# Output projection of three token blocks in rounded parts, and seven expert-table remainders moved to GpSimd, in an encoder block with a PEER expert layer

## The chip, the cores and the metric

The kernel runs on one core of a Trainium2 chip. The metric is the device time of one execution in microseconds (us), taken over several runs; a profile shows one more execution, instruction by instruction. The engines are named as in the profile: PE (TensorE, matmuls), DVE (VectorE), ACT (ScalarE), POOL (GpSimd) and SP (SyncE, which only issues transfers here).

## The reference

One encoder block on 512 tokens of width 1024: a mixer (a recurrent group with 8 heads in both directions and a short gated convolution with 4 channel groups), its output projection, a layer norm, a product-key expert layer (PEER), and a second layer norm.

```python
def reference(x, ...):
    h = layer_norm(x, ln_emb_g, ln_emb_b)
    z = h @ w_in
    xr, gate, cb, cc, cx = jnp.split(z, IN_SPLITS, axis=-1)
    ...
    y_lru = gelu(gate) * lru                      # 1024 channels
    y_conv = cb * depthwise_conv(cc * cx, conv_w) # 512 channels
    mix = jnp.concatenate([rms_norm(y_lru, norm_lru_g), rms_norm(y_conv, norm_conv_g)], -1)
    h = layer_norm(ALPHA * h + mix @ w_out, ln1_g, ln1_b)
    f = peer(h, peer_wq, peer_k1, peer_k2, peer_u, peer_v)
    h = layer_norm(ALPHA * h + f, ln2_g, ln2_b)

def peer(x, w_q, k1, k2, u_tab, v_tab):
    # per token and head (8 heads): the 16 best of 128 x 128 expert pairs, softmax g
    act = gelu(einsum("cd,ced->ce", x, u_tab[idx]))
    return einsum("ce,ced->cd", g * act, v_tab[idx])
```

## The kernel before, in words

The 512 tokens are four blocks of 128 (TB = 4). Everything is float32, but most products are made in rounded parts: a tile x is split into x_hi (x copied to the rounded matmul type by ACT) and x_lo (the remainder x - x_hi, also rounded, by DVE or POOL), and a product is a_hi b_hi + a_hi b_lo + a_lo b_hi, three rounded matmuls. The output projection is the exception: there `mm` takes the whole float32 tiles.

The program is four stages, each written as one list of instructions per engine; there is no scheduler, and each engine runs its list in order and waits on semaphores.

**Mixer** (`mixer`). For each of 28 column chunks of w_in: load (SP), upper part (ACT), remainder (POOL, `w_lower`, L401), 24 matmuls (`z_chunk`, L729). The results, 12 channel chunks, stand in `y` (chunks 0 to 7 are the heads, 8 to 11 the convolution; they are finished in the order `made`, convolution first). At the end of each head DVE runs two scans (L673), then POOL's `head_output` adds them, multiplies by the gate into `y` and squares (L409, L411, L416). The output projection (L772 to L791) goes block by block: 4 convolution chunks x 2 halves of 512 columns (L776), then 8 head chunks x 2 halves (L787); each matmul has a 128x128 piece of `y` as weights and 512 columns of `wo` as moving data. In block 0 it waits for the last head, and the sums of squares (L753, into bank 2) come before its last chunk. The mean squares go to DVE (L680) and POOL (L441). Block tb + 2 uses the banks of block tb, so it waits until DVE has added block tb's banks to `h` (L692, `o_used`); after that come statistics, POOL's root (L810, L812) and `normalise` (L557).

**Queries** (`queries`). The four blocks are turned into `xhi`, `xlo`; then 16 steps of one query chunk (24 matmuls, L1294), one block of 128 rows of the table U (128 blocks in all), and scores; 3 more steps have a U block only. A U block m: load into `u_raw` (4 buffers, L842), 8 transposes into PSUM (`turn`, L868), upper part by ACT (L897), remainder, 24 matmuls with 384 moving columns (`product`, L880), gelu, store. The transposes of block m + 1 stand ahead of the products of block m, and wait for the remainders of block m (each half for its bank). In this stage the remainder is made by POOL (`lower`, L920), which cannot read PSUM, so ACT writes a second, whole copy of each half (L900). DVE picks the top 16 of each score row meanwhile. The first four U blocks and the keys are loaded as soon as the mixer's buffers are free; the vectors `ln1_g`, `ln1_b` after the last block's `o_used`.

**Gates** (`gates`). 77 steps s, U block 19 + s each. Here the remainders are made by DVE straight from PSUM (`lower_pair`, L938). DVE also does the selection for each block (steps `SELECT_AT`: the far block 3 at 0 to 2, block 2 at 3 to 6, block 0 at 7 to 10, block 1 at 30 to 33), the one-hot tiles of two blocks (19 steps from 11 and from 43), and products of gathered rows. The far block is not made through the dense tables: POOL gathers its 128 rows per token of U and later of V (`GatherPath`, L1040, ring of 4 tiles), and DVE multiplies (`use`, L1052, L1056). `EARLY_USES` says how many of these uses stand in the query stage, `U_FROM` how many are done when the gate stage ends. From step 7 (`SCATTER_AT`) POOL also scatters the gates of block 2 to memory (L231). PE needs block 0's selection at the end of step 10.

**Experts** (`experts`). 128 steps over the table V with rounded parts (L1687), 32 of them with a U block as well; two gathered rows are used a step, later one. In step `WEIGH` (the first in which 128 uses are done) the gates are multiplied by the gelus and the two sums are cleared, and the uses of V rows begin.

## Time and profile before

| what | value |
|---|---|
| time of the kernel, median of 3 runs | 1699.42 us (1698.40 to 1699.64) |
| the profiled execution's own time | 1702.07 us |
| its span, first to last instruction | 1700.3 us |
| mean granted TensorE clock | 0.991 of full speed |
| PE busy | 96% |
| DVE busy | 74% |
| POOL busy | 49% |
| ACT busy | 38% |

Spans and times are of one execution. A matmul's record is longer than the distance to the next (they are pipelined), so costs of series are read from the chain of work or from the distance between starts. A whole float32 matmul leaves two records.

### The profile page before, as it was taken

How to read it: one execution, taken by the hardware profiler on the slowest of the kernel's cores; microseconds unless marked ns; L12 is line 12 of the kernel's file. 1: busy time of each engine (PE TensorE's matmuls, PEld its weight loads, DVE VectorE, ACT ScalarE, POOL GpSimd, SP SyncE). 2: the span in 40 equal slices, each digit the busy share in tenths (PEclk: the TensorE clock that was granted, in tenths of full speed). 3: DMA queues.
4: the chain of work that ended last, by engine and by line, in shares of the span. 5: the costliest groups of instructions: out<-in, count | busy, mean ns of one | idle time of the engine just before them, and what ended most of it. 6: DMA issues, size and time to landing. Idle time of an engine off the chain costs nothing.

```text
span 1700.3 us, 23332 instructions
## 1 busy us (share of the span) xinstructions
PE 1635.7 (96%) x8522; PEld 1418.6 (83%) x8522; DVE 1257.8 (74%) x2452; ACT 647.8 (38%) x1062; POOL 828.5 (49%) x542
## 2 busy tenths in 40 slices
PE   7998999899998999999999889999999999999997
PEld 5876644499998999999999888888888888888885
DVE  6567853388998898855886357778777877888876
ACT  3558750332433433432433233333333333333332
POOL 4734421274443378877877424445555563222200
PEclk9999999999999999999999999999999999999999
DMA  8436311133335578798779989998999989999973
GB/s 273 150 97 191 109 36 54 50 118 118 97 123 179 157 212 227 225 322 240 213 221 272 351 301 330 320 325 319 320 326 322 323 297 341 357 352 358 354 254 112
DMA packets 242896, 397.15 MB, mean 234 GB/s; under 512 B 33704, under 2 KB 173408, under 8 KB 242784
## 3 DMA queue, kind: packets, MB, share of 16 engines
q1 hardware_dynamic: 182816, 259.17, 44.8%
q0 software_dynamic: 55296, 134.31, 26.0%
q10 hardware_dynamic: 4672, 2.19, 0.5%
q8 instruction: 68, 1.11, 0.3%
q14 instruction: 44, 0.36, 0.1%
HBM read 349.40 MB, written 46.20 MB: 233 GB/s over the span
## 4 chain that ended last, share of the span: by engine, by line
PE 75%; DVE 14%; ACT 5%; DMA 2%; issue 2%; ACTq 1%; POOL 0%; SPq 0%; DVEq 0%; POOLq 0%
PE bank L1687 30%; PE bank L880 24%; PE bank L868 5%; PE bank L729 5%; PE bank L787 3%; PE bank L1561 3%; PE bank L1294 2%; DMA u_raw<-in_peer_u 2%; DVE dq L669 1%; PE bank L776 1%; DVE hd L673 1%; DVE sel_late L989 1%; ACT dw L536 1%; ACT da L538 1%; DVE ut_lo L938 1%
## 5 line engine op out<-in xcount | busy, mean ns | idle before, releaser
L880 PE MATMUL bank<-xhi,ut_hi 128*128 128x384 f32 x1024 | 354.8, 346 | 0.3 <-ACT gel L906 0.3
L880 PE MATMUL bank<-xhi,ut_lo 128*128 128x384 f32 x1024 | 344.7, 337 | 0.0
L880 PE MATMUL bank<-xlo,ut_hi 128*128 128x384 f32 x1024 | 344.0, 336 | 0.0
L1040 POOL DMA_INDIRECT gathered<-in_peer_v,expert_rows x128 | 198.2, 1549 | 261.5 <-DVE gather_sum L1056 242.6
L1040 POOL DMA_INDIRECT gathered<-in_peer_u,expert_rows x128 | 171.0, 1336 | 192.5 <-DVE gather_product L1052 167.0
L938 DVE TENSOR_TENSOR ut_lo<-bank,ut_hi 128x512 fp32r<-128x512 f32 x216 | 141.5, 684 | 154.4 <-ACT ut_hi L897 127.3
L231 POOL DMA_INDIRECT gate_matrix<-gate_values,gate_cells x128 | 221.1, 1728 | 56.5 <-issue 37.2
L1687 PE MATMUL bank<-v_hi,w_hi 128*128 128x512 f32 x760 | 237.7, 394 | 1.3 <-DVE w_lo L1799 1.3
L1687 PE MATMUL bank<-v_hi,w_lo 128*128 128x512 f32 x760 | 234.9, 390 | 0.0
L1687 PE MATMUL bank<-v_lo,w_hi 128*128 128x512 f32 x760 | 234.6, 390 | 0.0
L1732 ACT ACTIVATE v_hi<-gate_rows_then_feed 128x1024 fp32r<-128x1024 f32 x128 | 135.4, 1059 | 235.2 <-PE bank L1687 235.2
L1782 DVE TENSOR_TENSOR v_lo<-gate_rows_then_feed,v_hi 128x1024 fp32r<-128x1024 f32 x128 | 156.5, 1222 | 51.6 <-ACT v_hi L1732 51.6
L880 PEld LDWEIGHTS bank<-xhi,ut_hi 128*128 128x128 f32 x1024 | 193.8, 189 | 0.5 <-issue 0.5
L880 PEld LDWEIGHTS bank<-xlo,ut_hi 128*128 128x128 f32 x1024 | 193.9, 189 | 0.0
L880 PEld LDWEIGHTS bank<-xhi,ut_lo 128*128 128x128 f32 x1024 | 193.1, 189 | 0.0
L897 ACT ACTIVATE ut_hi<-bank 128x512 fp32r<-128x512 f32 x256 | 145.3, 604 | 84.6 <-PE bank L868 82.1
L1687 PEld LDWEIGHTS bank<-v_hi,w_lo 128*128 128x128 f32 x760 | 142.9, 188 | 30.0
L1687 PEld LDWEIGHTS bank<-v_lo,w_hi 128*128 128x128 f32 x760 | 142.9, 188 | 30.0
L1052 DVE SCALAR_TENSOR_TENSOR gather_product<-gathered,h 128x1024 f32<-128x1024 f32 x128 | 156.0, 1219 | 14.1 <-DMA gathered<-in_peer_u,expert_rows 9.6
L1687 PEld LDWEIGHTS bank<-v_hi,w_hi 128*128 128x128 f32 x760 | 140.8, 189 | 29.3 <-issue 1.7
L868 PE MATMUL bank<-ident,u_raw 128*128 128x128 f32 x1024 | 140.2, 275 | 23.6 <-DVE ut_lo L938 11.2
L1056 DVE SCALAR_TENSOR_TENSOR gather_sum<-gathered,expert_gates,gather_sum 128x1024 f32<-128x1024 f32 x128 | 160.5, 1278 | 0.3 <-DMA gathered<-in_peer_v,expert_rows 0.3
(212 smaller groups left out, 2515.2 us busy)
## 6 DMA issues: line engine op xcount, KB each, us to landing
u_raw<-in_peer_u SPq DMA_DIRECT2D x128, 512.0 KB
gate_rows_then_feed<-in_peer_v SPq DMA_DIRECT2D x128, 512.0 KB
gate_rows_then_feed<-gate_matrix SPq DMA_DIRECT2D x128, 192.0 KB
activations<-gel SPq DMA_DIRECT2D x96, 192.0 KB
gate_rows_then_feed<-activations SPq DMA_DIRECT2D x96, 192.0 KB
u_raw<-in_w_in SPq DMA_DIRECT2D x28, 512.0 KB, 4.1
gate_matrix<-gate_zeros SPq DMA_DIRECT2D x8, 1024.0 KB, 6.9
wq<-in_peer_wq SPq DMA_DIRECT2D x16, 512.0 KB, 4.6
```

What stands on the lines that cost most here:

```text
L231: self.nc.gpsimd.indirect_dma_start(out=self.flat, out_offset=bass.IndirectOffsetOnAxis(ap=self.at[:, k:k + 1], axis=0), in_=self.gate[:, ...
L729: ins = mm(z_bank(n)[:, :], w[n % 2][:, k, :], x[:, k, :], start=(i == 0), stop=(i == 3 * KD - 1))
L868: ins = self.nc.tensor.transpose(self.bank[b][:, k * P:(k + 1) * P], raw[:, j * P:(j + 1) * P], self.ident[:, :])
L880: ins = self.nc.tensor.matmul(self.bank[b + (r % 2) * spare][:, 0:DTOK], u[r % 2][:, k, :], x[:, k, 0:DTOK], start=(i == 0), stop=(i == 3 ...
L897: ins = self.nc.scalar.activation(self.hi[r % 2][at], turned, ACT.Copy)
L938: self.nc.vector.tensor_tensor(out=self.lo[r % 2][at], in0=self.bank[b].rearrange("p (k e) -> p k e", k=4), in1=self.hi[r % 2][at].bitcast ...
L1040: self.nc.gpsimd.indirect_dma_start(out=self.tile[r][:, :], out_offset=None, in_=self.tables[kind], in_offset=bass.IndirectOffsetOnAxis(ap ...
L1052: ins = V.scalar_tensor_tensor(out=self.product[:, :], in0=self.tile[r][:, :], scalar=1.0, in1=self.x, op0=ALU.mult, op1=ALU.mult, accum_o ...
L1056: ins = V.scalar_tensor_tensor(out=y, in0=self.tile[r][:, :], scalar=self.gate[:, k:k + 1], in1=y, op0=ALU.mult, op1=ALU.add)
L1687: ins = mm(bank[2 + 2 * tb + half][:, :], w[r][:, tb * P:(tb + 1) * P], v[r][:, half * HALF_D:(half + 1) * HALF_D], start=begins, stop=ends)
L1732: S.activation(v_hi[r][:, :], v_raw[r][:, :], ACT.Copy).then_inc(v_hi_ready, 1)
L1782: V.tensor_tensor(out=v_lo[r][:, :], in0=v_raw[r][:, :], in1=v_hi[r][:, :].bitcast(F32), op=ALU.subtract).then_inc(v_lo_ready, 1)
```

## The change

1. **Projection.** Blocks 1 to 3 are projected in rounded parts: ACT makes `wo_hi` and `y_hi` of each chunk (1024 and 384 columns), DVE's new `wo_lower` the remainders in place of `wo` and of blocks 1 to 3 of `y`. Block 0 stays whole, and so does one half of block 1's convolution chunks (`whole(1, 1, c, 1)`), which now stands ahead of block 0's heads. The upper parts lie in `xhi`, `xlo`, `ut_hi`, `ut_lo` and `u_raw`.
2. **Loads.** Since `u_raw` is in use, the first four U loads wait for the last block's `o_used`; they stand ahead of the loads of `ln1_g` and `ln1_b`. `prow` shares the buffer of `conv_products`, and its clearing waits for the transposes of `prow`.
3. **Gathers.** The query stage uses 4 gathered rows (`EARLY_USES` 2 and 2 instead of 2 and 4), the gate stage 71 instead of 70, the expert stage one more. With `U_FROM` odd, the use of the first V row falls into the step ahead of `WEIGH`, so the clearing of the sums drops that row's product (one of 128 per token of the far block).
4. **Remainders.** In steps 0 to 6 of the gate stage POOL makes the remainders (`lower`), ACT the second copies (`upper`).

```diff
-EARLY_USES = (0,) * (QC - 1) + (2, 4)
+EARLY_USES = (0,) * (QC - 1) + (2, 2)
...
+        eng.wait_ge(pT_ready, 1)
         G.memset(prods[:, :], 0.0).then_inc(prods_zero, 1)
...
+        for i, c in enumerate(made):
+            S.activation(wo_hi[c], wo[:, c, :], ACT.Copy).then_inc(wo_hi_ready, 1)
+            eng.wait_ge(y_ready, i + 1)
+            S.activation(y_hi[c], y[:, c, P:T], ACT.Copy).then_inc(y_hi_ready, 1)
...
+        def wo_lower(i):
+
+            eng.wait_ge(wo_hi_ready, i + 1)
+            eng.wait_ge(chunk_used, i + 1)
+            c = made[i]
+            V.tensor_tensor(out=wo_lo[c], in0=wo[:, c, :], in1=wo_hi[c].bitcast(F32),
+                            op=ALU.subtract).then_inc(wo_lo_ready, 1)
+            eng.wait_ge(y_hi_ready, i + 1)
+            eng.wait_ge(sq_ready, i + 1)
+            V.tensor_tensor(out=y_lo[c], in0=y[:, c, P:T], in1=y_hi[c].bitcast(F32),
+                            op=ALU.subtract).then_inc(y_lo_ready, 1)
+
+        for i in range(MIX // 2):
+            wo_lower(i)
         eng.wait_ge(sums_done, MIX)
...
         ins.then_inc(ms_ready, 1)
+        for i in range(MIX // 2, MIX):
+            wo_lower(i)
...
+            if tb == 1:
+                at = made.index(c) + 1
+                eng.wait_ge(wo_lo_ready, at)
+                eng.wait_ge(y_lo_ready, at)
+            tok = slice((tb - 1) * P, tb * P)
+            for ya, wb, begins, ends in ((y_hi[c][:, tok], wo_hi[c], first, False),
+                                         (y_hi[c][:, tok], wo_lo[c], False, False),
+                                         (y_lo[c][:, tok], wo_hi[c], False, last)):
+                for half in halves:
+                    ins = mm(out_bank(tb, i, half)[:, :], ya, wb[:, half * HALF_D:(half + 1) * HALF_D],
+                             start=begins, stop=ends)
...
+        for c in range(HEADS, MIX):
+            whole(1, 1, c, 1, c == HEADS, c == MIX - 1).then_inc(chunk_used, 1)
+        eng.wait_ge(factors_ready, 2 * HEADS)
...
+        mixed.out_used(eng, TB - 1)
         for m in range(UB):
             acts.load(eng, m, m)
-        mixed.out_used(eng, TB - 1)
...
         def gpsimd(eng):
             for s in range(STEPS):
+                if s < BY_POOL:
+                    acts.lower(eng, BY_QUERIES + s + 1, BY_QUERIES + s + 1)
                 for q in range(started_by(s), started_by(s + 1)):
                     far.start(eng, q)
```

On DVE, between the last head's scan and the first addition to `h`, before:

```order
L669 TENSOR_TENSOR dq<-dq,th 128x512
L673 SCALAR_TENSOR_TENSOR hd<-da,dq 128x512
L680 TENSOR_SCALAR rms<-bank 128x4 x2
L692 SCALAR_TENSOR_TENSOR h<-bank,rms,h 128x512 x4
L551 BN_STATS bn<-h 128x6 x2
```

The same place after (`wo_parts` and `y_parts` are the remainders, `ut_hi`, `xhi`, `y_hi`, `u_raw_parts` the places of the upper parts):

```order
L698 SCALAR_TENSOR_TENSOR hd<-da,dq 128x512
L708 TENSOR_TENSOR wo_parts<-wo,ut_hi 128x1024
L712 TENSOR_TENSOR y_parts<-y,y_hi 128x384
...
L708 TENSOR_TENSOR wo_parts<-wo,xhi 128x1024
L712 TENSOR_TENSOR y_parts<-y,u_raw_parts 128x384
L719 TENSOR_SCALAR rms<-bank 128x4 x2
L708 TENSOR_TENSOR wo_parts<-wo,xhi 128x1024
L712 TENSOR_TENSOR y_parts<-y,u_raw_parts 128x384
...
L733 SCALAR_TENSOR_TENSOR h<-bank,rms,h 128x512 x4
```

Six pairs now stand ahead of the mean squares and six between them and the first addition to `h`.

On POOL, from the last query remainders to the first scatters, before:

```order
L1230 TENSOR_TENSOR wq_lo<-wq,wq_hi 128x1024
L920 TENSOR_TENSOR ut_lo<-gather_sum,ut_hi 128x512 x4
L1040 DMA gathered<-in_peer_u,expert_rows 128x1024 x2
L920 TENSOR_TENSOR ut_lo<-gather_sum,ut_hi 128x512 x6
L1040 DMA gathered<-in_peer_u,expert_rows 128x1024 x5
L231 DMA gate_matrix<-gate_values,gate_cells 6291456x1 x6
```

The same place after:

```order
L1296 TENSOR_TENSOR wq_lo<-wq,wq_hi 128x1024
L986 TENSOR_TENSOR ut_lo<-gather_sum,ut_hi 128x512 x12
L1106 DMA gathered<-in_peer_u,expert_rows 128x1024 x4
L986 TENSOR_TENSOR ut_lo<-gather_sum,ut_hi 128x512 x12
L1106 DMA gathered<-in_peer_u,expert_rows 128x1024
L232 DMA gate_matrix<-gate_values,gate_cells 6291456x1 x6
```

Two gathers no longer stand among the query stage's remainders; four gathers now stand between the remainders of gate steps 0 and 1, and 14 halves of remainders (steps 0 to 6) are new.

## Rows read from the trace of the kernel before

**Rows 1.** The page: busy time by engine, and the chain by engine.
```profile
PE 1635.7 (96%) x8522; PEld 1418.6 (83%) x8522; DVE 1257.8 (74%) x2452; ACT 647.8 (38%) x1062; POOL 828.5 (49%) x542
PE 75%; DVE 14%; ACT 5%; DMA 2%; issue 2%; ACTq 1%; POOL 0%; SPq 0%; DVEq 0%; POOLq 0%
```
**Rows 2.** The chain of work, from 234 us: start, length, what (times and lengths in us).
```profile
234.45 12.28 PE bank L787 x28
248.41 1.82 PE bank L787 x4
...
298.31 13.75 PE bank L787 x32
...
588.77 4.17 PE bank L880 x24
...
749.21 0.87 PE bank L868 x8
...
1022.93 8.20 PE bank L1687 x36
```
**Rows 3.** Timeline of DVE: start, length, line, count, [idle before, releaser].
```profile
118.04 0.69 DVE L669 TENSOR_TENSOR dq<-dq,th 128x512 f32<-128x512 f32 x1 [0.93 <-ACT dq L495]
...
119.91 2.78 DVE L669 TENSOR_TENSOR dq<-dq,th 128x512 f32<-128x512 f32 x1
...
239.01 1.22 DVE L673 TENSOR_TENSOR_SCAN hd<-da,dq 128x512 f32<-128x512 f32 x1
...
250.81 2.85 DVE L692 SCALAR_TENSOR_TENSOR h<-bank,rms,h 128x512 f32<-128x512 f32 x4 [2.13 <-POOL rms L441]
...
549.34 2.29 DVE L980 TENSOR_TENSOR hit_late<-placef_late,iotab_late 128x2048 bf16<-128x2048 bf16 x1
...
1209.10 1.22 DVE L1782 TENSOR_TENSOR v_lo<-gate_rows_then_feed,v_hi 128x1024 fp32r<-128x1024 f32 x1
1210.23 0.55 DVE L1799 TENSOR_TENSOR w_lo<-w,w_hi 128x384 fp32r<-128x384 f32 x1
1210.70 0.69 DVE L938 TENSOR_TENSOR ut_lo<-bank,ut_hi 128x512 fp32r<-128x512 f32 x1
```
**Rows 4.** Timeline of POOL, the same columns.
```profile
119.48 2.66 POOL L403 TENSOR_TENSOR ut_lo<-u_raw,ut_hi 128x1024 fp32r<-128x1024 f32 x1 [11.16 <-ACT ut_hi L469]
...
240.37 1.26 POOL L409 TENSOR_TENSOR hd<-hd 128x512 f32<-128x512 f32 x1 [10.51 <-DVEq L676]
...
248.76 2.01 POOL L441 TENSOR_TENSOR rms<-rms,small 128x4 f32<-128x4 f32 x2 [4.67 <-DVE rms L680]
...
331.22 2.49 POOL L920 TENSOR_TENSOR ut_lo<-gather_sum,ut_hi 128x512 fp32r<-128x512 f32 x2 [13.72 <-ACT gather_sum L900]
...
529.15 1.88 POOL L1040 DMA_INDIRECT gathered<-in_peer_u,expert_rows  x1 [2.13 <-DVE gather_product L1052]
...
534.00 0.94 POOL L1040 DMA_INDIRECT gathered<-in_peer_u,expert_rows  x1 [0.30 <-issue]
```
**Rows 5.** Timeline of ACT: its first work behind the mixer's heads.
```profile
252.76 1.06 ACT L1200 ACTIVATE wq_hi<-wq 128x1024 fp32r<-128x1024 f32 x1 [15.90 <-DMA wq<-in_peer_wq]
```
**Rows 6.** Transfers issued from 313 to 331 us: KB each, us to landing.
```profile
ln<-in_ln_b SPq DMA_DIRECT2D x1, 512.0 KB, 5.5
wq<-in_peer_wq SPq DMA_DIRECT2D x1, 512.0 KB, 6.6
```
**Rows 7.** Timeline of PE: the projection's start, and the waits where the gate stage opens.
```profile
226.64 7.03 PE L776 MATMUL bank<-wo,y 128*128 128x512 f32 x16
...
516.82 0.63 PE L868 MATMUL bank<-ident,u_raw 128*128 128x128 f32 x4 [0.79 <-POOL ut_lo L920]
...
538.11 1.94 PE L868 MATMUL bank<-ident,u_raw 128*128 128x128 f32 x8 [5.22 <-DVE ut_lo L938]
```
**Rows 8.** Busy time by stretch: PE, PEld, DVE, ACT, POOL, then granted clock, DMA share, GB/s.
```profile
538.00:541.00 3.00, 2.89 (x12) 2.92 (x13) 2.93 (x4) 1.19 (x2) 0.00 (x0) 0.50 0.84 338
...
600.00:995.00 395.00, 384.81 (x2563) 381.13 (x2563) 274.93 (x588) 138.03 (x325) 287.06 (x187) 1.00 0.89 256
```

80 lines of the change are left out of this document (52 added, 28 removed).

## The prediction

> **What bounds the kernel now.** I read the page first: PE is busy 96% of the span and holds 75% of the chain [rows 1]. So a change pays where it shortens PE's own work or takes away one of its few waits. Then I read the chain around the projection and the gate stage [rows 2], the timelines of the engines that feed PE there [rows 3, 4], and PE's waits [rows 7]. The reader should see three things. From 234.45 to 312.05 us PE does almost nothing but whole float32 matmuls, back to back [rows 2]. From 516 us, where the gate stage opens, it waits for remainders, above all 5.22 us at 538.11 [rows 7]. And the granted clock is at the lower level (0.50 of 2.4 GHz, so 1.2 GHz) right behind that wait [rows 8].
>
> All times below are in the old trace's coordinates. Where both changes act, the later one simply starts earlier by what the first one gained, since the query stage starts when the projection ends and nothing in it hangs on an absolute time.
>
> **1. The matmuls of the projection.** 32 records are 16 whole matmuls in 13.75 us, 0.859 us each [rows 2]. The same form in rounded parts (128x128 weights, 512 moving columns, two halves on one weight tile) takes 8.20 us for 36, 0.228 us each, three of them 0.683 [rows 2]. So a matmul saves 0.176 us. Changed are 24 in block 2, 24 in block 3, 20 in block 1: 68 x 0.176 = 11.9 us. The four whole matmuls that are pulled ahead of block 0's heads (3.4 us) use up PE's wait of 0.8 us for the last factors of the heads: the convolution part of block 0 ends at 226.64 + 7.03 = 233.7, the heads' part begins at 234.45 [rows 2, 7]. Ideal: 12.7 us.
>
> **2. The remainders on DVE, and who waits.** A 1024-column remainder starts 1.13 us before the next instruction, a 384-column one 0.47 us (1209.10, 1210.23, 1210.70) [rows 3]: 1.60 a pair, 12 pairs, 19.3 us. They can start when DVE's last scan ends, at 240.2. ACT is free from 236.9 (15.90 us before 252.76), and its 1024-column copy takes 1.06 us [rows 5], the 384-column one less, so ACT stays ahead. Block 0 ends at 248.41 + 1.82 [rows 2] + 3.4 - 0.8 = 252.9 us.
>
> There is a catch. A DVE instruction with two SBUF inputs that met a POOL one (start 119.48, end 122.14) took 2.78 us instead of 0.69: it was over 0.55 us after POOL's end [rows 3, 4]. The two alternate. The first six pairs meet POOL's three instructions of `head_output` from 240.37 on (1.26 us the first [rows 4], 3.6 in all), so they end at 240.2 + 9.6 + 3.6 = 253.4; with the mean squares about 253.8. PE may open block 1 (whose bank 2 holds them) 0.9 us late. The other six pairs meet POOL's roots (2.01 us [rows 4]): 253.8 + 9.6 + 2.0 = 265.4. Inside block 1 PE needs 2.7 us for the convolution halves and 1.37 us for each head chunk, DVE 1.60 to 1.9; DVE is two chunks ahead when it begins, and its last remainder (265.4) is due at 253.8 + 2.7 + 7 x 1.37 = 266.1. No stall, but no more than 0.7 us of room. Block 1 ends at 267.4. Then block 2 waits for DVE's addition of block 0, 2.85 us, which stood at 250.81 [rows 3] and now is queued behind the pairs: 265.4 + 2.9 = 268.3, so 0.9 us more. Later additions fit (a block takes 16.4 us on PE). Projection: 12.7 - 1.8 = **10.9 us** saved. Bounds: without any collision 12.7; with each DVE instruction at its full record (1.22 + 0.55 = 1.77 a pair) two more, 8.9.
>
> The Trainium skill speaks against both halves of the change here: "GPSIMD Engine Reference", Key points, says that GpSimd shares its SBUF interfaces with VectorE and contends with instructions that have two SBUF inputs. By it the new pairs contend, and the gate remainders, which DVE took from PSUM, become contending ones on POOL. The trace agrees with it for the pair at 119.48. Without the rule the projection would give its 12.7.
>
> **3. Loads.** The four U loads now wait for the last `o_used`, which comes 2.9 us after the projection's end, at 315. PE needs the first of them, and POOL the norm vectors, shortly before POOL's remainder at 331.22 [rows 4]. Two of the loads issued there, 0.5 us apart, landed 5.5 and 6.6 us after issue, 1.6 us apart [rows 6]. With four more in front the U blocks land by 325 and the vectors by 327. Cost nothing, under the projection's tail (norm, turn, first query chunk); 4 us of room. The `prow` wait and the one gathered row more in the gate and expert stages lie under other work (DVE is busy 74% [rows 1]).
>
> **4. Opening of the gate stage.** A step of PE is 8 transposes and 24 products, 0.87 + 4.17 = 5.04 us [rows 2]. From 516.0 (the start of the first wait, step for U block 17) to the end of the products of gate step 10 (588.77 + 4.17 = 592.9) stand 13 steps: ideal 65.5, taken 76.9. So 11.4 us are lost, to the waits and to the slow clock. What is late next, after the change? Two gathers no longer stand ahead of the remainder for which PE waits at 516.82 [rows 7] and for its second half: 1.3 us back. DVE no longer carries 14 halves there (0.69 us each [rows 3], 9.7 us) nor two uses, and PE no longer waits for its list, so the 5.22 us wait goes. But POOL's four gathers (529.15 to 534.94, 5.8 us [rows 4]) now stand between the remainders of steps 0 and 1. They would start at 531, and the next remainder (2.5 us for both halves) ends at 539.2. PE wants its second half in its fifth step, at 516.0 + 4 x 5.04 + 0.9 = 537.1: 2.1 us late. DVE's 2.29 us comparison [rows 3] can hold a half back; a half takes two copies and a POOL half, some 3.7 us behind its transposes, so PE's slack is about 1.2 us and each meeting costs up to 1.1, in two or three steps; and ACT, with four copies a step, loads another table in steps 0 and 3. I take 1.6 us for these two, and 0.5 for the selection from step 7 on, where DVE makes the remainders again. Sum lost 4.2, gained 11.4 - 4.2 = **7.2 us**. Bounds: 11.4 (nothing waits), 3 (each of the seven steps loses 1.2 us).
>
> **Sum**: 10.9 + 7.2 = 18.1 us of the profiled execution's 1700.3 us span; its own time is 1702.07, 2.6 above the median of the runs. Taken from the median: 1699.4 - 18.1 = 1681.3.
>
> **Rivals.**
> (a) *All of it pays*: no contention, no POOL lag, 12.7 + 11.4 = 24.1: 1675.3. For it: DVE and POOL alternate only when they meet. Against: DVE's pairs and POOL's first instruction are released by the same scan, and POOL's stood at 240.37 [rows 4].
> (b) *The opening gives nothing*: POOL's remainders come as late as DVE's did, the gathers and ACT's tables included. 1699.4 - 10.9 = 1688.5. Against: in the query stage POOL's two halves take 2.5 us of a step of 5.04 there as well, and PE is held only where gathers stand among them.
> (c) *The U loads come late*: they share the queue with the vectors and the first query weights. At 3 us a load instead of 1.5 the vectors land at 336, 5 us late: 1686.3.
> (d) *The later part takes it back*: from 600 to 995 us the transfers are busy 0.89 [rows 8]; if they were the true bound, arriving 18 us earlier would turn into waits, up to half: 1690. Against: PE is busy 384.8 of 395 us there, and transfers are issued by its progress.
> (e) *Slower*: PE's clock. A wait of 5.22 us was followed by the lower level, and the 0.79 us at 516.82 was not (an estimate from PE's records, which keep their length there). If POOL leaves PE a gap in every one of steps 1 to 7 and the clock stays at 1.2 GHz there, each step costs 5.0 us more: 35 - 18 = 17 us slower, 1716. It decides only if short repeated gaps bring the clock down.
> (f) *The change doesn't do what it says* can be left at a per cent: the lists of the engines show the new order.
>
> **How the numbers follow.** Forecast as summed (1677 to 1686) 0.63; (a) 0.11; (b) 0.11; (c) 0.06; (d) 0.05; (e) 0.03; (f) 0.01. The likeliest is 1681.3. The range runs from (a) to just past (b), 1675.0 to 1688.7; (d) and (e) are left out. A measurement can tell about 0.2% (3.4 us) from no change. Only (e), (f) and the far end of (d) are not faster by that: faster 0.94, same 0.03, slower 0.03.
>
> **What would show it right or wrong.** The projection's rounded matmuls at 0.228 us and its end near 301 us; DVE's pairs at 1.6 us with POOL's three instructions between them; waits of about a microsecond before block 1 and block 2. The first U transposes without a wait for a load. At the gate stage's opening, PE waiting for POOL once for about 2 us (behind the four gathers), the clock at 1.00 throughout, and step 10's products ending near 575 us in the new trace (592.9 - 18.1). It would be wrong if the pairs take 2 us or more, if the U loads are the releaser of PE's first transposes, or if the waits from 600 us on grow well beyond what PE loses there now (10 us of 395).

## The result, and the profile after

The changed kernel takes 1692.99 us (median of 20 runs, 1687.06 to 1697.96) beside 1702.37 us for the kernel before on the same chip (20 runs, 1698.4 to 1709.28). The ratio is 0.9945, 95% interval 0.9936 to 0.9955: 9.4 us faster (7.7 to 10.9). The forecast was 18.1 us faster and a range that ended at 1688.7. The sign was right, the size is half, and the time lies outside the range. Part of the distance in absolute time is the base: the forecast was taken from a median of 3 runs of the kernel before, 1699.42, and 20 runs give 1702.37, 3.0 us more. What the change itself does is read from the difference.

The profiled execution has a span of 1689.5 us against 1700.3, 10.8 us less. The page, busy time and the chain by engine, as [rows 1] of before:

```profile
PE 1626.1 (96%) x8590; PEld 1433.5 (85%) x8590; DVE 1280.3 (76%) x2462; ACT 671.7 (40%) x1100; POOL 854.1 (51%) x556
PE 79%; ACT 6%; DVE 6%; DMA 3%; issue 3%; POOL 2%; SPq 1%; ACTq 0%; DVEq 0%; POOLq 0%
```

PE has 9.6 us less to do (1635.7 before), and that is nearly all that the span lost. The forecast's other half, waits that go away, is nearly absent.

**The projection.** Timeline of PE (start, length, instructions, and in brackets the idle time before them and who ended it), then the chain of waits for the same place (start, length, what), then two stretches (PE, PEld, DVE, ACT, POOL busy, granted clock, DMA share, GB/s):

```profile
249.52 1.45 PE L815 MATMUL bank<-wo,y 128*128 128x512 f32 x3
253.63 0.63 PE L829 MATMUL bank<-ut_hi,y_hi 128*128 128x512 f32 x1 [2.66 <-DVE rms L719]
```
```profile
253.63 49.04 PE bank L829 x204
```
```profile
253.60:257.40 3.80, 3.77 (x10) 2.96 (x11) 3.80 (x5) 1.91 (x2) 3.74 (x1) 0.55 0.91 214
257.40:302.60 45.20, 45.20 (x197) 36.66 (x196) 25.21 (x32) 0.00 (x0) 14.62 (x10) 1.00 0.00 1
```

The rounded part opens at 253.63 (forecast: 253.8), but PE has then stood idle for 2.66 us, and the first nine matmuls run at the lower level of the clock, 0.43 us apart. The last of the 204 ends at 302.67, where the whole ones of [rows 2] ended at 312.05: 9.4 us saved between these two profiles, not 10.9.

What DVE and POOL did meanwhile (L708 and L712 are the remainders of `wo` and `y`, L719 the mean squares, L733 the addition to `h`; on POOL L427 to L434 are the end of the last head, L460 the roots):

```profile
240.74 2.28 DVE L708 TENSOR_TENSOR wo_parts<-wo,ut_hi 128x1024 fp32r<-128x1024 f32 x1 [0.21 <-PE bank L815]
242.94 1.63 DVE L712 TENSOR_TENSOR y_parts<-y,y_hi 128x384 fp32r<-128x384 f32 x1
244.50 2.06 DVE L708 TENSOR_TENSOR wo_parts<-wo,ut_hi 128x1024 fp32r<-128x1024 f32 x1
246.48 0.55 DVE L712 TENSOR_TENSOR y_parts<-y,y_hi 128x384 fp32r<-128x384 f32 x1
246.95 1.21 DVE L708 TENSOR_TENSOR wo_parts<-wo,ut_lo 128x1024 fp32r<-128x1024 f32 x1
...
253.36 0.22 DVE L719 TENSOR_SCALAR rms<-bank 128x4 f32<-128x4 f32 x2
...
265.12 2.85 DVE L733 SCALAR_TENSOR_TENSOR h<-bank,rms,h 128x512 f32<-128x512 f32 x4 [1.91 <-POOL rms L460]
```
```profile
242.02 2.15 POOL L429 TENSOR_TENSOR y<-y,hd 128x512 f32<-128x512 f32 x1
...
253.66 11.42 POOL L460 TENSOR_TENSOR rms<-rms,small 128x4 f32<-128x4 f32 x2 [8.18 <-DVE rms L719]
```

The first three remainders meet POOL's instructions and take 2.28, 1.63 and 2.06 us in place of 1.21 and 0.55; from the fourth on a pair takes 1.61 us. And POOL's two tiny root instructions, 2.01 us in [rows 4], last 11.42 us: they end at 265.08, 1.9 us behind DVE's last pair (263.20), so they look as if they had been served only then.

**The opening of the gate stage.** Timeline of PE, then of POOL (L986 remainders, L1106 gathers), of ACT (L1076 the exponent and its table, L963 and L966 the two copies) and of DVE (L1046, L1053 and, not shown here, L1055: comparison, product and reduction of one piece of the selection), then a stretch:

```profile
529.47 0.63 PE L934 MATMUL bank<-ident,u_raw 128*128 128x128 f32 x4 [2.55 <-POOL ut_lo L986]
530.60 1.11 PE L934 MATMUL bank<-ident,u_raw 128*128 128x128 f32 x4 [0.50 <-POOL ut_lo L986]
...
544.74 0.66 PE L934 MATMUL bank<-ident,u_raw 128*128 128x128 f32 x4 [2.37 <-POOL ut_lo L986]
...
575.22 1.16 PE L934 MATMUL bank<-ident,u_raw 128*128 128x128 f32 x8 [0.39 <-DVE ut_lo L1004]
```
```profile
518.46 3.58 POOL L986 TENSOR_TENSOR ut_lo<-gather_sum,ut_hi 128x512 fp32r<-128x512 f32 x2 [2.52 <-ACT gather_sum L966]
522.19 0.97 POOL L1106 DMA_INDIRECT gathered<-in_peer_u,expert_rows  x1
...
526.35 1.69 POOL L1106 DMA_INDIRECT gathered<-in_peer_u,expert_rows  x1 [0.30 <-issue]
528.06 2.49 POOL L986 TENSOR_TENSOR ut_lo<-gather_sum,ut_hi 128x512 fp32r<-128x512 f32 x2
...
540.13 4.56 POOL L986 TENSOR_TENSOR ut_lo<-gather_sum,ut_hi 128x512 fp32r<-128x512 f32 x2 [5.94 <-ACT gather_sum L966]
```
```profile
537.48 1.28 ACT L1076 ACT_TABLE_LOAD   x1
538.77 0.31 ACT L1076 ACTIVATE ex_late<-ex_late 128x128 f32<-128x128 f32 x1
538.99 0.58 ACT L963 ACTIVATE ut_hi<-bank 128x512 fp32r<-128x512 f32 x1
```
```profile
540.28 3.29 DVE L1046 TENSOR_TENSOR hit_late<-placef_late,iotab_late 128x2048 bf16<-128x2048 bf16 x1
543.60 2.17 DVE L1053 TENSOR_TENSOR hit_late<-hit_late,keyf_late 128x2048 bf16<-128x2048 bf16 x1
```
```profile
529.50:533.00 3.50, 3.00 (x13) 2.76 (x14) 3.25 (x8) 2.17 (x4) 2.52 (x3) 0.62 1.01 378
```

The wait of 5.22 us for DVE [rows 7] is gone. In its place PE waits 2.55 + 0.50 us for POOL, behind the four gathers, and the clock falls to the lower level all the same (0.62 on average over 3.5 us; the step's products take 5.17 us instead of 4.17 in the chain). Three steps later it waits 2.37 us more, for a pair of halves that took POOL 4.56 us where 2.49 stand above.

**One table for all that follows.** PE transposes one block of U at a time, and the starts of these transposes (the rows `bank<-ident,u_raw`) are marks that every kernel here has. The first two blocks, which lie 3.3 us apart, are counted together as 0. In the trace after, numbers 16 and 30 are the rows that start at 501.45 and 580.73, and number 97 is the second half of its block, at 995.74, behind a wait of 4.11 us. Number 16 lies three blocks ahead of the gate stage's step 0, number 30 starts right behind the products of its step 10 (the stretch of the forecast's 11.4 us and one step more), number 97 is the last mark before the experts. All times in us:

| kernel | start of 0 | 16 to 30 | 30 to 76 | 76 to 97 | span | ratio (95%) |
|---|---|---|---|---|---|---|
| before | 329.3 | 82.3 | 286.5 | 127.8 | 1700.3 | 1 |
| changed | 319.9 | 79.3 | 285.5 | 129.4 | 1689.5 | 0.9945 (0.9936 to 0.9955) |
| changed_again | 320.1 | 77.0 | 290.7 | 124.2 | 1689.0 | 0.9938 (0.9919 to 0.9956) |
| proj_only | 319.1 | 79.8 | 286.2 | 132.5 | 1692.9 | 0.9948 (0.9927 to 0.9969) |
| proj_again | 319.0 | 79.6 | 286.0 | 129.7 | 1691.5 | 0.9962 (0.9950 to 0.9974) |
| gate_only | 330.3 | 79.3 | 286.3 | 124.4 | 1695.4 | 1.0005 (0.9991 to 1.0019) |
| ms_after_4 | 317.1 | 81.2 | 288.5 | 128.3 | 1691.9 | 0.9949 (0.9934 to 0.9965) |
| gathers_spread | 319.1 | 78.5 | 286.7 | 129.9 | 1690.9 | 0.9928 (0.9907 to 0.9950) |
| long_proj | 331.1 | 81.1 | 289.2 | 124.4 | 1701.2 | 1.0002 (0.9988 to 1.0015) |
| pool_none | 319.7 | 76.9 | 288.2 | 132.9 | 1693.5 | 0.9949 (0.9929 to 0.9969) |
| exp_behind | 318.8 | 77.0 | 287.9 | 124.7 | 1682.7 | 0.9923 (0.9906 to 0.9940) |
| all_three | 317.1 | 76.5 | 286.1 | 132.5 | 1687.5 | 0.9907 (0.9887 to 0.9927) |
| pool_3 | 319.1 | 77.4 | 287.2 | 126.0 | 1683.7 | 0.9928 (0.9913 to 0.9943) |
| two_pool | 317.9 | 74.0 | 285.8 | 129.2 | 1682.5 | 0.9910 (0.9894 to 0.9925) |
| none_ms | 316.2 | 78.4 | 287.1 | 130.4 | 1686.6 | 0.9942 (0.9926 to 0.9959) |
| short_48 | 308.6 | 82.9 | 289.4 | 130.7 | 1685.8 | 0.9908 (0.9894 to 0.9923) |
| long_144 | 352.4 | 81.2 | 289.5 | 124.4 | 1722.5 | 1.0164 (1.0144 to 1.0183) |

Read down a column before you read along a row. The columns of stretches come from one profiled execution each, the ratio from several runs. The last stretch swings by 8.7 us between kernels whose code there is nearly the same, so a span alone tells little; from 97 to the end it is 692.4 to 694.5 us in all of them. Between changed and before, the start of transpose 30 is 12.4 us earlier, of transpose 97 11.7, the end 10.8. Every kernel with four early gathers drops the same product of one V row as the change does.

### The profile page after: what moved, and what is told of

It is laid out like the page before. It is cut to its first block, busy times and chain, and to the rows that moved or that the text cites. A ratio compares the mean times of both kernels' runs of the same rounds, so it can differ in the third digit from the quotient of the medians.

```text
span 1689.5 us, 23564 instructions
## 1 busy us (share of the span) xinstructions
PE 1626.1 (96%) x8590; PEld 1433.5 (85%) x8590; DVE 1280.3 (76%) x2462; ACT 671.7 (40%) x1100; POOL 854.1 (51%) x556
## 3 DMA queue, kind: packets, MB, share of 16 engines
q10 hardware_dynamic: 4672, 2.19, 0.5%
## 4 chain that ended last, share of the span: by engine, by line
PE 79%; ACT 6%; DVE 6%; DMA 3%; issue 3%; POOL 2%; SPq 1%; ACTq 0%; DVEq 0%; POOLq 0%
PE bank L1756 30%; PE bank L946 26%; PE bank L934 6%; PE bank L1357 5%; PE bank L770 5%; PE bank L1630 3%; PE bank L829 3%; DMA u_raw<-in_peer_u 2%; DVE dq L694 1%; DVE hd L698 1%; PE bank L1345 1%; POOL ut_lo L986 1%; ACT dw L555 1%; ACT da L557 1%; ACT th L552 1%
## 5 line engine op out<-in xcount | busy, mean ns | idle before, releaser
L1106 POOL DMA_INDIRECT gathered<-in_peer_v,expert_rows x128 | 195.1, 1525 | 264.1 <-DVE gather_sum L1122 245.1
L1004 DVE TENSOR_TENSOR ut_lo<-bank,ut_hi 128x512 fp32r<-128x512 f32 x202 | 132.6, 684 | 155.2 <-ACT ut_hi L963 143.8
L1106 POOL DMA_INDIRECT gathered<-in_peer_u,expert_rows x128 | 171.6, 1340 | 153.9 <-DVE gather_product L1118 127.2
L232 POOL DMA_INDIRECT gate_matrix<-gate_values,gate_cells x128 | 216.3, 1690 | 61.3 <-issue 37.2
L1851 DVE TENSOR_TENSOR v_lo<-gate_rows_then_feed,v_hi 128x1024 fp32r<-128x1024 f32 x128 | 156.4, 1222 | 43.9 <-ACT v_hi L1801 41.2
L963 ACT ACTIVATE ut_hi<-bank 128x512 fp32r<-128x512 f32 x256 | 146.0, 604 | 84.4 <-PE bank L934 81.8
L1118 DVE SCALAR_TENSOR_TENSOR gather_product<-gathered,h 128x1024 f32<-128x1024 f32 x128 | 156.0, 1219 | 16.7 <-DMA gathered<-in_peer_u,expert_rows 12.4
```

The source lines that it names most:

```text
L232: self.nc.gpsimd.indirect_dma_start(out=self.flat, out_offset=bass.IndirectOffsetOnAxis(ap=self.at[:, k:k + 1], axis=0), in_=self.gate[:, ...
L963: ins = self.nc.scalar.activation(self.hi[r % 2][at], turned, ACT.Copy)
L1004: self.nc.vector.tensor_tensor(out=self.lo[r % 2][at], in0=self.bank[b].rearrange("p (k e) -> p k e", k=4), in1=self.hi[r % 2][at].bitcast ...
L1106: self.nc.gpsimd.indirect_dma_start(out=self.tile[r][:, :], out_offset=None, in_=self.tables[kind], in_offset=bass.IndirectOffsetOnAxis(ap ...
L1118: ins = V.scalar_tensor_tensor(out=self.product[:, :], in0=self.tile[r][:, :], scalar=1.0, in1=self.x, op0=ALU.mult, op1=ALU.mult, accum_o ...
L1851: V.tensor_tensor(out=v_lo[r][:, :], in0=v_raw[r][:, :], in1=v_hi[r][:, :].bitcast(F32), op=ALU.subtract).then_inc(v_lo_ready, 1)
```

## The experiments

**The two parts apart.** proj_only is the change without its gate stage (`U_FROM = 76`, `EARLY_USES` 2 and 4, no remainder of the gate stage on POOL, the two gathers in the query stage); gate_only is the kernel before with that part alone:

```diff
-U_FROM = 76
+U_FROM = 75
-EARLY_USES = (0,) * (QC - 1) + (2, 4)
+EARLY_USES = (0,) * (QC - 1) + (2, 2)
+BY_POOL = SCATTER_AT
...
-            if m == QC:
-                for q in range(RING, U_QUERIES):
-                    far.start(eng, q)
...
+                if s < BY_POOL:
+                    acts.lower(eng, BY_QUERIES + s + 1, BY_QUERIES + s + 1)
```

> The projection in parts and the later U loads alone; the gate stage and the gathers as before. Theory (the two parts are independent, and the projection's gain is what its stage shows): the first query chunk starts 9.4 us earlier than before, the gate stage keeps its old losses (one wait of about 5 us for DVE, clock at the lower level behind it), and the whole is 9 to 9.5 us faster, 1690 to 1693 against 1700 to 1702. Rival (what is gained early is given back later, by transfers that are busy 0.9 from 600 us on): less than 6 us faster although the first query chunk starts 9.4 us earlier.

> The four uses in the query stage and POOL's seven remainders alone, on the kernel before; the projection as before. As in the changed kernel, the first gathered V row's product of the far block is dropped. Theory: PE's wait of 5 us at the opening goes, two waits of about 2.5 us for POOL (behind the four gathers in step 1, behind ACT's table loads in step 3) come in its place, the clock falls behind the first; 3 us faster at step 10 and 1 to 3 us in all. Rival (my forecast): 7 us faster. Rival (given back by the transfers): no difference at the end.

The projection alone gives 0.9948 and, once more, 0.9962: 8.8 and 6.5 us. The gate stage's part alone gives nothing that can be measured, 1.0005 (1.5 us faster to 3.2 slower). proj_only was expected to give 9 to 9.5 us and proj_again a ratio of 0.994 to 0.995; the second missed that (0.9962, 0.9950 to 0.9974; more on its base below). So the projection is most or all of the result, and the gate stage's part, from which 7.2 us were expected, is where the forecast went wrong. (The two proj ratios together, 0.9959, leave 2.6 us to the 0.9943 of changed and changed_again together, with an interval of 0.3 to 5.0; gate_only says 0. A gain of a microsecond or two is not excluded, 7.2 is.) How wrong shows in the column 16 to 30. The three profiles with the old arrangement of remainders (before, proj_only, proj_again) have 82.3, 79.8 and 79.6 us, mean 80.6. The seven with the new one and no other edit of the stage (changed, changed_again, gate_only, ms_after_4, long_proj, short_48, long_144) have 77.0 to 82.9, mean 80.3. The one profile of the kernel before, from which the forecast read its loss, is the worst of the three: it has waits of 0.79 and 0.50 us at 516.8 (proj_only and proj_again: one of 0.34) and 6.8 us at the lower clock where they have 3.4. The trace of proj_again still has the old wait in full, at 527.70:

```profile
527.70 1.94 PE L934 MATMUL bank<-ident,u_raw 128*128 128x128 f32 x8 [5.19 <-DVE ut_lo L1004]
```

**Who makes the remainders.** pool_none and pool_3 are the changed kernel with one number changed, `BY_POOL = 0` and `BY_POOL = 3` in place of 7: none or three steps of remainders on POOL; the two uses of gathered rows stay moved.

> The changed kernel with all remainders of the gate stage on VectorE as before (GpSimd takes none of the seven steps), and the four early gathers and two uses of gathered rows moved as in the change. Theory, from the traces so far (gate opening 79.8 us with the old arrangement and 79.3 with the new one, from U transpose 16 to 30): the arrangement hardly matters, so this is within 1 us of the changed kernel, 0.993 to 0.996 of before; the trace shows the single wait of 4 to 5 us on VectorE's ut_lo again and no wait over 1 us on GpSimd. Rival (the prediction's: GpSimd's share of the work is worth 7 us): 5 us or more slower than the changed kernel, 0.997 or more of before.

> The changed kernel with GpSimd taking the first three remainders of the gate stage and not seven. It shares with the changed kernel the four gathers between its remainders. If contention with VectorE's comparisons is what makes GpSimd's remainders late (theory): the wait of 2.4 us at the fourth step goes, the one of 2.55 us at the second stays, and transposes 16 to 30 take 76.5 to 78 us against 79.3 in the changed kernel. Rival (GpSimd must take all seven, since VectorE is late with each that it keeps): a wait on VectorE's ut_lo of 1.5 us or more appears behind the third step, and 16 to 30 take 79 us or more. At the end 0 to 2.5 us faster than the changed kernel, 0.992 to 0.995 of before.

```profile
524.64 0.66 PE L934 MATMUL bank<-ident,u_raw 128*128 128x128 f32 x2 [3.07 <-DVE ut_lo L1004]
```

The rival (5 us slower) fell, and the theory missed the size of the wait: without any help from POOL the opening takes 76.9 us, no more than with it (80.3 on average, 77.0 to 82.9) and less than the old arrangement (79.7 in the two proj kernels). The row shows one reason: with two uses less ahead of it (1.2 us each on DVE) the wait for DVE has shrunk from 5.19 to 3.07 us by itself, here and in none_ms (below), the other kernel without POOL's help, alike. The two take 76.9 and 78.4 us, 2.1 less than the proj kernels, which fits. That POOL's share on top takes this back (80.3) is likely from the waits that come with it, but seven profiles of that arrangement spread over 5.9 us, and two without it don't prove a loss; nothing in them or in the times points to a gain from POOL's share. pool_3 takes 77.4: the wait behind the gathers stays (2.55 us at 528.64), the one three steps later is gone, and no wait on DVE over 0.4 us has come for it. That is what its theory said, and the rival fell. In the whole time pool_none equals the changed kernel (0.9949), and pool_3's 0.9928 is 2.6 us better, which can't be told from nothing.

**The gathers and the exponent.** gathers_spread starts the four gathers one a step in steps 1 to 4, not all in step 0; exp_behind issues ACT's exponent of the third selection behind the copies of its step:

```diff
-    started_by = lambda s: min(U_FROM, used_by(s) + RING) if s else U_QUERIES
+    started_by = lambda s: min(U_FROM, used_by(s) + RING, U_QUERIES + max(s - 1, 0) if s <= RING else U_FROM)
```
```diff
-                if part == 0 and tb != DT:
+                early = tb == DT or s < BY_POOL
+                if part == 0 and not early:
                     picks.exponent(eng, nth[tb] + 1, QH)
...
-                if part == 0 and tb == DT:
-                    picks.exponent(eng, nth[tb] + 1, heads_of(DT)[1])
+                if part == 0 and early:
+                    picks.exponent(eng, nth[tb] + 1, heads_of(DT)[1] if tb == DT else QH)
```

> The changed kernel with POOL's four gathers of the gate stage's opening spread over steps 1 to 4, one behind each step's remainders, instead of four behind step 0's; it drops the same V row. Theory (these gathers hold up the remainder of step 1 by 5.8 us; the wait of 2.55 us and the lower clock behind it follow from that): the wait at 529.5 goes or falls under 1 us, the clock stays up, step 10 ends 3 to 5 us earlier. The wait of 2.4 us at 544.7 stays. 3 to 4 us faster than the changed kernel. Rival (DVE's selection is the limit of this stretch anyway): the waits only move to later steps, under 1 us in all.

> The changed kernel with ScalarE's exponent of the third selection issued behind the upper copies of its step and not ahead of them. In the changed kernel's trace the table load and exponent stand at 537.5 to 539.1 ahead of the copies, and TensorE then waits 2.37 us at 544.74 for GpSimd's remainder. Theory A (the exponent delays that remainder): the wait at that step goes from 2.4 us to under 1, and U transpose 25 starts 1.5 to 2.5 us earlier against transpose 16 than in the changed kernel. Theory B (VectorE's comparison and GpSimd's subtraction slow each other, 4.56 us for the pair at 540.13 where 2.5 stand elsewhere): the wait stays at 1.5 us or more, and nothing is gained. In the whole time at most 2.5 us, which five rounds hardly tell from nothing.

> The changed kernel once more, beside the three others, for more executions and a second profile of it. Up to the end of the gate opening it should repeat its first profile within 1 to 2 us. Question of this run: between U transposes 76 and 97, where VectorE waits for gathered rows, profiles of kernels with the same code there differ by up to 7 us so far. If that is chance from one execution to the next, this profile takes other waits there than the first one (129.4 us from 76 to 97 in the first) although nothing differs; if it is the code, it repeats 129.4 within 1 us. The ratio should be 0.9945 within 0.002.

Spreading the gathers cut the first wait from 2.55 to 1.12 us, but four others of 0.36 to 1.49 us came behind it, all for POOL's remainders; 16 to 30 take 78.5 us, the clock fell all the same (0.63 in the 3.5 us behind the second of them), and 0.9928 against 0.9945 can't be told from nothing (expected: 3 to 4 us).

exp_behind did what theory A said: no wait at the fourth step, 77.0 us, 0.9923. The other profiles with the change's arrangement all wait there but one (2.37 us in changed and gate_only, two waits of together 3.1 to 3.2 us in ms_after_4, long_proj, short_48 and long_144). Yet that one, changed_again, the change word for word, shows that a single profile is no proof, here or for pool_3. There the exponent still stands ahead of the copies (537.80), and the wait is 0.36 us, not 2.37. The timelines of changed_again, PE, POOL and DVE:

```profile
543.03 0.66 PE L934 MATMUL bank<-ident,u_raw 128*128 128x128 f32 x4 [0.36 <-POOL ut_lo L986]
```
```profile
540.46 2.52 POOL L986 TENSOR_TENSOR ut_lo<-gather_sum,ut_hi 128x512 fp32r<-128x512 f32 x2 [4.80 <-ACT gather_sum L966]
```
```profile
539.75 2.29 DVE L1055 TENSOR_REDUCE sel_late<-hit_late 128x128 f32<-128x2048 bf16 x1
542.07 3.05 DVE L1046 TENSOR_TENSOR hit_late<-placef_late,iotab_late 128x2048 bf16<-128x2048 bf16 x1
```

The remainder began 0.3 us later than in the first profile and ended 1.7 us earlier, because it ran beside DVE's reduction, which has one input, and met the comparison only with its last 0.9 us: 2.52 us, not 4.56. So 2.0 of the 2.4 us were the meeting (theory B), and whether it happens is decided by a microsecond or two from one execution to the next (the pair began 0.3 us later, the comparison 1.8). At the end of the stage changed_again was at 77.0 us, the changed kernel at 79.3, with the same code. How much moving the exponent brings by itself stays open.

**Better arrangements.** ms_after_4 moves the mean squares on DVE ahead of the fifth pair of remainders, so that PE can open block 1 sooner:

```diff
-        for i in range(MIX // 2):
+        for i in range(CONV):
             wo_lower(i)
...
-        for i in range(MIX // 2, MIX):
+        for i in range(CONV, MIX):
             wo_lower(i)
```

none_ms is that with `BY_POOL = 0`; all_three is ms_after_4, gathers_spread and exp_behind together; two_pool is all_three with `BY_POOL = 2`. That number also takes the exponent's edit out again: it acts only in the steps that POOL has, and the third selection's exponent stands in step 3.

> The changed kernel with the mean squares behind four of the twelve pairs of remainders on DVE instead of six; it drops the same V row. Theory (PE's wait of 2.7 us before block 1 and the lower clock of the 3.8 us behind it are the price of the two pairs too many): the wait goes, block 1 starts at about 251 us with the clock at the upper level, its rounded matmuls at 0.232 us from the first; block 1 ends 4 us earlier (265), and then block 2 waits for DVE's addition of block 0, which still comes at 265 to 268, so 2 to 3 us of it are lost again, and the clock may fall there; net 1 to 2 us faster than the changed kernel. Rival (the wait is harmless, the pairs themselves are the limit): the projection ends where it did, at 302.7, and the time is the same.

> The changed kernel with no remainder of the gate stage on GpSimd, the two uses of gathered rows moved as in the change, and all four convolution chunks' remainders ahead of the mean squares. The projection should then end 2 to 3 us earlier than in the changed kernel (first query matmul at 308.7 to 309.5 us; TensorE's clock 1.00 in 250 to 260 us), transposes 16 to 30 take 76.9 us against 79.3. If the later stages hand this on: 4 to 5 us faster than the changed kernel, 0.991 to 0.993 of before. If the stretch bound by transfers takes it back: under 1 us, 0.994 to 0.995.

> The changed kernel with three edits at once: the order of mean squares and remainders on VectorE (all four convolution chunks' remainders before the mean squares), the gathers spread over the steps, and the exponent behind the copies. If the waits add up as the traces show them one by one (2.7 us at the start of block 1, 3.7 and 2.4 us in the gate stage): 4 to 7 us faster than the changed kernel, 0.990 to 0.992 of before. If each wait that goes is followed by another that was hidden behind it (VectorE's selection work up to U transpose 30): no more than 2 us faster, 0.993 to 0.995.

> The kernel with the three edits (remainders of the convolution chunks ahead of the mean squares, gathers spread over the steps, exponent behind the copies), but with GpSimd taking only the first two remainders of the gate stage. Theory (GpSimd is worth having only where VectorE works through the first selection; later it is slowed by VectorE's comparisons and slows them): transposes 16 to 30 take 73.5 to 75.5 us against 76.5 with all seven, and the whole is 1 to 3 us faster than that, 0.989 to 0.990 of before. Rival (the opening is bound by VectorE's selection work whichever engine takes remainders): 76 us or more, and no difference from the kernel with the three edits, 0.9907 of before.

Timeline of PE and a stretch of ms_after_4 (in the changed kernel, profiled again, the same stretch has the clock at 0.83 and PE busy 7.34 us):

```profile
252.31 0.47 PE L829 MATMUL bank<-ut_hi,y_hi 128*128 128x512 f32 x1 [0.30 <-DVE y_parts L712]
```
```profile
250.00:260.00 10.00, 9.70 (x39) 7.02 (x39) 9.78 (x15) 4.84 (x6) 3.54 (x2) 1.00 0.66 171
```

PE's wait shrinks from 2.66 to 0.30 us, the clock stays at its upper level (2.4 GHz), and the first transpose comes on average 2.3 us earlier in the four kernels with this edit (316.2 to 317.9 against 318.8 to 320.1 in the eight without the edit and without added or left-out matmuls). That reading is safe. The loss that was expected at block 2 did not come: DVE's addition of block 0 started at 263.20 (265.12 in the changed kernel), because POOL's roots took 3.54 us and not 11.42. In the whole time the edit alone brought nothing that can be seen (0.9949; expected: 1 to 2 us); its one profile has a slow opening, 81.2 us. none_ms missed its 4 to 5 us too (0.9942).

all_three reaches 0.9907 (expected: 0.990 to 0.992) and two_pool 0.9910; against 0.9945 and 0.9938 for the changed kernel that is some 6 us, and the intervals lie apart (at most 0.9927, against at least 0.9934 for the changed kernel's two results together; changed_again alone, from six runs, overlaps). Both beat both kernels, by 15.5 us the kernel before. two_pool has the shortest opening of all, 74.0 us as expected, with the upper clock throughout:

```profile
520.00:540.00 20.00, 18.55 (x119) 18.06 (x118) 19.21 (x28) 10.66 (x18) 8.80 (x8) 1.00 0.62 215
```

and yet it isn't faster than all_three (expected: 1 to 3 us); 2.5 us in the opening are no more than the other stretches' swings (0.9910 within 0.0016). In all_three POOL goes on making remainders beside DVE's comparisons. The worst meeting there, POOL and DVE:

```profile
538.79 5.39 POOL L986 TENSOR_TENSOR ut_lo<-gather_sum,ut_hi 128x512 fp32r<-128x512 f32 x2 [0.38 <-ACT gather_sum L966]
```
```profile
540.87 2.19 DVE L1053 TENSOR_TENSOR hit_late<-hit_late,keyf_late 128x2048 bf16<-128x2048 bf16 x1
```

POOL's pair 5.39 us for 2.5, DVE's product 2.19 for 1.23.

**Does what is gained early arrive at the end?** Three kernels change only how long the projection takes (the diff is long_144's; long_proj has the inner loop once). long_proj and long_144 do the first part of block 3 two and four times over, short_48 leaves out the products with remainders in block 3:

```diff
+            if tb == TB - 1:
+                for _ in range(3):
+                    for c in range(HEADS):
+                        in_parts(tb, 0, c, (0, 1), c == 0, c == HEADS - 1)
```

> The changed kernel with the 48 rounded matmuls of token block 3's first part done twice (the second time starts the sum anew, so that nothing else changes). It asks what a microsecond of the projection is worth at the end. By the changed kernel's own pace of 0.2317 us a matmul the first query matmul should start 11.1 us later. If the later stages hand everything on (theory of the prediction): the whole kernel takes 10.5 to 11.5 us more than the changed one, which is 1.001 to 1.002 of the kernel before. If the stretch in which transfers are busy 0.9 of the time absorbs part of every shift (rival d): the difference between U transposes 57 and 60, where TensorE waits for U loads, shrinks, and the whole takes only 6 to 9 us more, 0.998 to 1.000 of before.

> The changed kernel in which token block 3's projection leaves out the two products with remainders (48 matmuls fewer; its rows of h are therefore rounded ones). By 0.2317 us a matmul everything behind starts 11.1 us earlier. If the later stages hand on every shift and the 3 us between the opening and the end are chance: 10 to 11.5 us faster than the changed kernel, 0.987 to 0.989 of before. If transfers set a floor under the stretch behind the opening: transposes 30 to 97 take 419 us or more on this profile and the kernel gains 7 us or less, 0.990 or more.

> The changed kernel with token block 3's first part of the projection done four times in place of once: 144 matmuls more, 33.4 us. If every shift is handed on: 32.5 to 34 us slower than the changed kernel, 1.0135 to 1.0145 of before. If an early arrival costs a part of itself (0.27 us for each us, by the profiles so far): 24 to 27 us slower, 1.0085 to 1.0105, and transposes 30 to 97 take 408 to 411 us. If the loss is a step that ends once the arrival is as late as before's: about 30 us slower, 1.0115 to 1.0125, and 412 to 414 us for 30 to 97.

> The kernel with the projection's part of the change alone, once more, beside the two others. Its first profile had 79.8 us for transposes 16 to 30 and 132.5 for 76 to 97, its ratio was 0.9948 within 0.0021. If what varies between profiles behind the opening is chance, 76 to 97 take 124 to 130 us this time. The ratio should be 0.994 to 0.995; were it 0.997 or more, the gate stage's part of the change would be worth 3 us after all.

Against the changed kernel's two ratios together (0.9943 within 0.0009, the mean by their intervals; times 1701): an arrival 11.3 us earlier gave 6.0 us less (3.1 to 8.9), 11.2 us later gave 10.0 more (7.3 to 12.7), 32.5 us later 37.6 more (33.9 to 41.2). From end to end that is 43.6 us for 43.8. So over the whole width a microsecond in the projection is worth a microsecond at the end, and the slope of 0.73 that the profiles had suggested before these runs is refuted. For an early arrival alone, which is what rival (d) is about, the numbers are less clear. short_48 lost 5.3 of its 11.3 us, and proj_again came 10.3 us earlier than the kernel before and gave 6.5. But these two and long_144, which came out 5.1 us too slow, ran on one chip beside a kernel before of 1698.21 us, 2 to 4 us faster than in the runs of the others. All three being some 4 to 5 us too slow points to that base, since a floor under early arrivals would have spared long_144; compared with each other they go one for one. long_proj and changed_again, both on another chip, do too (10.9 us for 11.0). The base is the likelier reading, and it is argued, not shown; for short_48 the profile has another place for part of it, the opening (82.9 us, the longest of all, with waits of 2.52, 1.65 and 1.48 us for POOL and the lower clock for 10.2 us).

What stays open: the last stretch, 76 to 97, where PE and DVE wait for transfers. The longest wait in proj_only, on DVE, for a gathered row (proj_again has 2.8 us less in that stretch, with the same code):

```profile
875.04 1.22 DVE L1118 SCALAR_TENSOR_TENSOR gather_product<-gathered,h 128x1024 f32<-128x1024 f32 x1 [6.28 <-DMA gathered<-in_peer_u,expert_rows]
```

changed and changed_again differ by 5.2 us there (129.4, 124.2) and by as much, the other way, from 30 to 76. Over all 17 profiles 30 to 97 take 413.1 us on average where transpose 30 comes later than 590 us (4 profiles, 410.7 to 414.3) and 416.6 where it comes before 582 (13, 412.6 to 421.1). A loss of about 3 us for an early arrival, a small part of rival (d), may be real, but no slope goes with it, and no run isolates it.

## Why the prediction was half right

**What bounds the kernel: right.** PE's own work was the place to save: 9.6 us less busy time stand beside 9.4 us less in the runs.

**Step 1, the matmuls: right but for the pace.** 195 rounded matmuls at the upper clock take 45.2 us, 0.232 each, not the 0.228 of the experts' form in [rows 2]. Over 204 that is 0.8 us. The wait of 0.78 us before block 0's heads was used up as said.

**Step 2, DVE: the times right, one consequence missed.** Block 1 opens at 253.63 (said: 253.8), a pair takes 1.61 us (1.60), the first three remainders alternate with POOL's instructions as said. Missed was what PE's idleness costs beside itself: PE began the projection at 224.91 in this profile (226.64 before; 223.7 to 226.8 over all 17), so block 0 ended at 251.0 and not 252.9, the wait is 2.66 us and not 0.9, and behind it nine matmuls ran at 1.2 GHz, 1.8 us. In short_48, which has the same code up to block 3, PE began at 226.78 and block 1 opened as forecast, with the clock at 1.00 from 253.60 to 257.40:

```profile
253.62 0.50 PE L829 MATMUL bank<-ut_hi,y_hi 128*128 128x512 f32 x1 [0.85 <-DVE rms L719]
```

The forecast priced the clock's fall for seven steps in rival (e) only, and not in its sum. The second collision came out the other way round: I charged 2.0 us to DVE for POOL's roots, and DVE lost nothing while POOL's 2.01 us became 11.42. "GPSIMD Engine Reference", Key points, in the Trainium skill says that the two engines contend for the shared SBUF interfaces where DVE has two SBUF inputs; the trace agrees, and adds who loses when DVE has a row of such instructions back to back. It was harmless by luck: the addition of block 0 came at 265.12 (said: 265.4) and ended 1.2 us before block 2, itself late by the cold start, wanted its bank. Sum of the projection in this pair of profiles: 10.9 + 0.2 (earlier opening) + 0.9 (no wait at block 2) - 1.8 (clock) - 0.8 (pace) = 9.4. Over more profiles the forecast stands better: the first transpose starts at 329.3 and 330.3 us with the old projection and at 319.4 on average in the eight profiles named above, 10.4 us earlier.

**Step 3, loads: right.** PE's first transposes followed without a wait for a load; the first came 9.4 us earlier, the projection's gain and nothing else.

**Step 4, the gate opening: the step that failed.** It promised that POOL's taking of the remainders would win back 7.2 of 11.4 us, 4.2 being lost to what comes next. Forecast 7.2 us; in the first profile 3.0 (82.3 to 79.3), over ten profiles 0.3 (80.6 to 80.3), in the runs of gate_only -0.9 (-3.2 to 1.5). Its terms:
- *What was lost before*, 11.4 us, was read from one profile, the worst of three; the other two lose 2.6 less.
- *The four gathers*, 2.1 us: measured 2.55 + 0.50, and then the slow clock, 1.0 us of products and a slower transpose. From transpose 20 to 22 the kernel takes 15.1 us where two steps are 10.1: 5.0, not 2.1 (in changed_again, with the same waits and the clock at 1.00, 3.5). The sentence "the clock at 1.00 throughout" was the mistake: [rows 8] had shown what follows a wait of 5 us, and I took a shorter wait to be free of it.
- *POOL meeting DVE's comparison*, 1.6 us with the tables: 2.6 us in the first profile; in changed_again 0.6 at this step and 1.3 at two later ones. The price of 2.5 us for POOL's pair was taken from [rows 4], where DVE has no bf16 comparison beside it. Beside one, or beside the selection's product, it was 4.56 and 5.39 us, and the comparison itself 3.29 for 2.29. The prediction had applied such a meeting to the projection's pairs in numbers, but here only as "can hold a half back".
- *The selection from step 7 on*, 0.5 us: measured 0.6. With 5.0 and 2.6 that makes 8.2 us lost in the first profile, not 4.2.
- Left out was that the old wait could be had away without POOL: two uses moved take 2.1 of its 5.2 us.

**The rivals.** (b), that the opening gives nothing, came nearest, with a chance of 0.11 and for the reason it named (POOL's remainders come as late as DVE's did). Its 1688.5 us lay 4.5 us too low: 3.0 of them are the base of 1699.42 us, and 1.5 its 10.9 us for the projection, where the whole kernel gained 9.4. (d) is refuted as a slope; a loss of about 3 us for early arrivals stays open. (e), the clock, was real as a mechanism: two short falls, some 3 us, not seven steps. The range ended just past (b), at a gain of 10.7 us. Its own lower bound for the projection, 8.9 us, together with (b) would have held the gain of 9.4, but not the time, for which the base had to be right as well.

**The whole miss.** The time missed by 1692.99 - 1681.3 = 11.7 us, of which 3.0 are the base. The gain missed by 18.1 - 9.4 = 8.7 us: 1.5 in the projection, 4.2 in the opening and 1.6 behind it (12.4 us at transpose 30, 10.8 at the end, 0.9 of it behind transpose 97) in the profiles; the last 1.4 is the difference between one pair of profiles and the medians. The waits from 600 us on did not grow: in the same code, 12 us earlier, PE idles 10.3 of 386 us where it idled 10.2.

## What to carry to other kernels

Moving work from a late engine to an idle one pays only for what the idle one can do undisturbed: price its instructions from rows where the other engine does what it will do then, and first ask whether the queue ahead of the wait can be shortened instead. Beside a wait of PE of a few microseconds, price the matmuls at half speed that can follow it: 1.8 us behind the 2.66 us here, and behind shorter waits less often (counts below). Take what a stretch loses, and the base that the gain is subtracted from, from more than one profile and more than three runs before promising to win it back.

## What the runs showed of the hardware

- Behind a wait of 2.66 us PE's clock was at its lower level (0.55 of full speed in the 3.8 us behind it), behind 2.55 + 0.50 us too (0.62 over 3.5 us); behind 0.30 and 0.85 us at the same place in other profiles it stayed at 1.00. Over all 17 profiles, from 245 to 1675 us, for waits that began at full speed: behind all 27 of 3.0 to 6.2 us the mean clock of the next 3.5 us was below 0.95, behind neither of two of 2.72 and 2.81 us, behind 15 of 17 of 2.5 to 2.7 us, behind 13 of 61 of 1.6 to 2.0 us, behind 8 of 31 of 1.4 to 1.6 us. Short waits are thus not safe either: three waits of 1.69, 1.83 and 1.46 us behind the projection left the clock at 1.00 in the kernel before and ended with 0.54 from 311.60 to 315.20 in the changed one. With the same code and the same waits (2.55 and 0.50) the mean clock of 520 to 540 us was 0.91 in one profile and 1.00 in another (changed and changed_again): a wait of this length is followed by the fall mostly, not always.
- Two POOL instructions of 4 columns, 2.01 us before, took 11.42 us beside a row of twelve DVE instructions with two SBUF inputs without a gap, and ended 1.9 us behind it. With four pairs ahead of the mean squares and eight behind, the same two took 3.54 us. Why there a gap was found early stays open.
- POOL's pair of 512-column subtractions: 2.49 to 2.55 us alone, and 2.52 beside DVE's reduction with one input; 3.58 beside DVE's two products of gathered rows (518.46), 4.56 and 5.39 beside the selection's comparison and product.
- Rounded matmuls of 512 columns, three products to a chunk: 0.232 us apart in the projection, 0.228 in the experts.
